# A two-layer attention and state-space step on one Trainium2 core: three gating blocks taken in turns, and the S5 read-out placed later among the weight units

## What is computed

```python
def _s5_layer(x, cond, p, init, return_state):
    h, gate = _pre(x, cond, g, w_ada, b_ada)
    u, z = jnp.split(h @ w_in, 2, axis=-1)
    ...
    hfr, hfi = _s5_scan(ug, a_re[0], ...)             # forward in time
    hbr, hbi = _s5_scan(ug[:, ::-1], a_re[1], ...)    # backward in time
    y = _s5_readout(hfr, hfi, ...) + _s5_readout(hbr, hbi, ...)[:, ::-1]
    y = y.reshape(bsz, l, D_MODEL) + d_skip * uf
    y = jax.nn.gelu(y)
    y = y * jax.nn.sigmoid(y @ w_glu + b_glu)         # the gating product
    out = (y * jax.nn.silu(z)) @ w_out
    x_new = x + gate * out
```

## Time and profile before

| | |
|---|---|
| median of 3 runs | 1264.6 us (1262.93 to 1269.76) |
| profiled execution | 1265.03 us, of which its span 1263.2 us |
| busy share of the span | PE 89%, DVE 60%, ACT 46%, POOL 18% |
| mean granted clock of PE | 0.942 of full speed |
| the chain that ended last | PE 65%, DVE 15%, DMA 9%, ACT 7%, issue 3% |

### The profile page before, as it was taken

How to read it: one execution, slowest core, us unless ns; L and a number is a source line. 1 busy time by engine, 2 the same in 40 slices (tenths; PEclk the granted TensorE clock), 3 DMA queues, 4 the chain that set the end, 5 groups by cost and what they waited for, 6 DMA issues and landing times.

```text
span 1263.2 us, 17442 instructions
## 1 busy us (share of the span) xinstructions
PE 1125.0 (89%) x6802; PEld 846.3 (67%) x6802; DVE 762.2 (60%) x1285; ACT 576.0 (46%) x808; POOL 222.1 (18%) x386
## 2 busy tenths in 40 slices
PE   4776999999999999999899969999697968799994
PEld 0224677677777777888667657788586856687883
DVE  3004776566656665787588745379676974365554
ACT  1313534434343444445434354565658475254443
POOL 2000222034202230331232230221020202100000
PEclk9866999999999999999999979999798978899998
DMA  9996789688969895666788775787272936754551
GB/s 355 422 394 250 261 319 336 258 335 320 349 256 347 311 354 204 209 219 214 286 336 330 289 269 207 244 289 241 105 262 90 298 106 231 270 196 167 178 189 66
DMA packets 60034, 327.21 MB, mean 259 GB/s; under 512 B 8800, under 2 KB 11616, under 8 KB 27952
## 3 DMA queue, kind: packets, MB, share of 16 engines
q1 hardware_dynamic: 38816, 262.44, 55.8%
q0 software_dynamic: 14224, 53.16, 12.3%
q10 hardware_dynamic: 6912, 10.49, 2.3%
HBM read 295.65 MB, written 30.41 MB: 258 GB/s over the span
## 4 chain that ended last, share of the span: by engine, by line
PE 65%; DVE 15%; DMA 9%; ACT 7%; issue 3%; ACTq 0%; SPq 0%; POOL 0%; DVEq 0%
PE ps L703 17%; PE ps L705 16%; PE ps L704 16%; DMA raw<-in_wada 6%; PE ps L601 5%; DVE wlo L1339 4%; DVE sb L1443 4%; DVE t L1438 3%; ACT whi L968 2%; PE ps L812 1%; PE ps L660 1%; PE ps L688 1%; PE ps L645 1%; DMA raw<-in_w 1%; PE ps L841 1%
## 5 line engine op out<-in xcount | busy, mean ns | idle before, releaser
L1339 DVE TENSOR_TENSOR wlo<-raw,whi 128x1024 fp32r<-128x1024 f32 x288 | 352.2, 1226 | 358.3 <-ACT whi L968 354.9
L968 ACT ACTIVATE whi<-raw 128x1024 fp32r<-128x1024 f32 x288 | 303.5, 1058 | 484.9 <-PE ps L705 469.5
L703 PE MATMUL ps<-whi,xhi 128*128 128x512 f32 x1152 | 477.3, 414 | 3.5 <-DVE xlo L1358 3.5
L704 PE MATMUL ps<-wlo,xhi 128*128 128x512 f32 x1152 | 456.2, 396 | 0.0
L705 PE MATMUL ps<-whi,xlo 128*128 128x512 f32 x1152 | 456.1, 396 | 0.0
L703 PEld LDWEIGHTS ps<-whi,xhi 128*128 128x128 f32 x1152 | 221.2, 192 | 78.5 <-issue 20.3
L705 PEld LDWEIGHTS ps<-whi,xlo 128*128 128x128 f32 x1152 | 220.4, 191 | 49.0
L704 PEld LDWEIGHTS ps<-wlo,xhi 128*128 128x128 f32 x1152 | 221.2, 192 | 46.2 <-issue 3.9
L601 PE MATMUL ps<-raw,cT 128*32 128x512 f32 x256 | 52.6, 929 | 31.7 <-DMA raw<-in_wada 31.5
L1443 DVE TENSOR_TENSOR sb<-sb,t 128x128 f32<-128x128 f32 x256 | 69.0, 290 | 6.6
L601 PE MATMUL ps<-araw,cT 128*32 128x512 f32 x512 | 61.5, 598 | 0.0
(11 more groups left out here) (205 smaller groups left out, 1077.1 us busy)
## 6 DMA issues: line engine op xcount, KB each, us to landing
raw<-in_w SPq DMA_DIRECT2D x144, 1024.0 KB, 5.0
araw<-in_wada SPq DMA_DIRECT2D x64, 1024.0 KB, 8.3
raw<-in_wada SPq DMA_DIRECT2D x32, 1024.0 KB, 8.7
btab_scratch<-bs ACTq DMA_DIRECT2D x32, 256.0 KB, 4.2
ctab_scratch<-ce POOLq DMA_DIRECT2D x16, 512.0 KB, 7.2
btab<-btab_scratch SPq DMA_DIRECT2D x16, 512.0 KB, 4.3
ctab<-ctab_scratch POOLq DMA_DIRECT2D x16, 512.0 KB, 4.7
par<-in_par POOLq DMA_DIRECT2D x32, 128.0 KB, 6.0
```

The source lines that it names most:

```text
L703: mm(acc, xhi[:, kt, st], whi[:, s, k], start=kt == 0, stop=False)
L704: mm(acc, xhi[:, kt, st], wlo[:, k0 // 2 % 4, k0 % 2, k], start=False, stop=False)
L968: af(whi[:, k % 4].rearrange("p k c -> p (k c)"), src, ACT.Copy).then_inc(s_hi, 1)
L1339: tt(wlo[:, g % 4, k % 2].rearrange("p k c -> p (k c)"), src, whi[:, k % 4].rearrange("p k c -> p (k c)").bitcast(F32), ALU.subtract).then ...
```

## The change

The budget's rules change in two numbers: the `hy` copies of a group start two units behind its last scan step, not one, and the sums of group w + 2 start four units behind those copies (`k + 6`, where the copies are at `k + 2`), not one. The gating blocks 28, 29 and 30 are taken in turns of two units. Block 30 then needs two more banks of PSUM while 28 and 29 hold theirs: it gets banks 4 and 5, slices 0, 1 and 2 of `Y` pass through banks 5, 7 and 4, the slices behind them all through bank 7, and every read-out uses bank 6 (those of groups 2 and 3 used bank 4, as the transposed final states did). Waits are adapted to that.

Worked out from the code, the tables of units are:

| | before | after |
|---|---|---|
| first sums, w = 0 to 3 | 176, 184, 197, 207 | 176, 184, 201, 209 |
| first `hy` copies | 196, 206, 219, 227 | 197, 205, 222, 230 |
| first read-out | 200, 210, 222, 230 | 201, 209, 225, 233 |
| transposes of slices 3 to 7 | 226, 230, 231, 234, 235 | 226, 231, 233, 238, 240 |
| unit that needs slices 3 to 7 | 229, 232, 233, 236, 237 | 231, 236, 237, 242, 243 |
| last scan step | 226 | 228 |
| steps of two groups at once / alone | 32 / 64 | 24 / 80 |

```diff
-B_PAIR = B_GLU
+B_TURNS = B_GLU
@@ scan_plan
                 if done[w] == NCH:
-                    ends[w] = k + 1
+                    ends[w] = k + 2
                     if w + 2 < NW:
-                        sums[w + 2] = k + 2
+                        sums[w + 2] = k + 6
@@
-X_AT = {226: 3, 230: 4, 231: 5, 234: 6, 235: 7}
-YZ_AT = (230, 231, 235, 236)
+X_AT = {226: 3, 231: 4, 233: 5, 238: 6, 240: 7}
+YZ_AT = (230, 231, 236, 241)
@@ place
-    j = k - UB * B_PAIR
-    if 0 <= j < 2 * UB:
-        return B_PAIR + j // 2 % 2, 2 * (j // 4) + j % 2
+    j = k - UB * B_TURNS
+    if 0 <= j < 3 * UB:
+        return B_TURNS + j // 2 % 3, 2 * (j // 6) + j % 2
@@ new functions
+def acc_bank(b):
+    return 4 if b == B_TURNS + 2 else 2 * ((b + (b > B_TURNS + 2)) % 2)
+
+def x_bank(n):
+    if n // TG == STAGES.index(B_TURNS):
+        return (5, 7, 4)[n % TG] if n % TG < AHEAD else 7
+    return 5 + n % 3
@@ PE, transposed
                 if g >= AHEAD:
-                    pe.wait_ge(s_xlo, n - AHEAD + 1)
+                    pe.wait_ge(s_xlo, n - AHEAD + 1 if i != 3 else n - 1 if g == AHEAD else n)
@@ PE, unit
-                if u == 0 and b >= 2:
-                    wait_evacuated(pe, b - 2)
+                if u == 0 and b == B_TURNS + 2:
+                    pe.wait_ge(s_xlo, TG * STAGES.index(B_TURNS) + AHEAD)
+                elif u == 0 and b >= 2:
+                    wait_evacuated(pe, b - 3 if b in (B_TURNS + 3, B_TURNS + 4) else b - 2)
@@ PE, ahead of the gating and of the output blocks
                 if u == 0 and b == B_GLU:
                     pe.wait_ge(s_uTsb, 2 * NW)
                     pe.wait_ge(s_Ssb, 4 * 4 * NW)
-                    pe.wait_ge(s_ysb, 8)
+                if u == 0 and b == B_OUT1:
+                    wait_evacuated(pe, B_TURNS + 2)
+                    pe.wait_ge(s_fso, 1)
```

More of the change, by code:

```diff
@@ L148, in ahead @@
     b, u = k // UB, k % UB
-    if b in (B_PAIR, B_PAIR + 1):
+    if B_TURNS <= b < B_TURNS + 3:
         return (X_AT[k],) if k in X_AT else ()
     return (u + AHEAD,) if b in STAGES and u + AHEAD < TG else ()
+def acc_bank(b):
[4 more added lines that the diff above has]
+    return 5 + n % 3
 def stage(k):
@@ L684, in transposed @@
                 if g >= AHEAD:
-                    pe.wait_ge(s_xlo, n - AHEAD + 1)
+                    pe.wait_ge(s_xlo, n - AHEAD + 1 if i != 3 else n - 1 if g == AHEAD else n)
                 for k in range(2):
                     for st in range(NS):
-                        last = tr(ps[:, 5 + n % 3, (2 * k + st) * P:(2 * k + st + 1) * P],
+                        last = tr(ps[:, x_bank(n), (2 * k + st) * P:(2 * k + st + 1) * P],
                                   src[:, st, (2 * g + k) * P:(2 * g + k + 1) * P], ident[:])
@@ L701, in unit @@
                     for st in range(NS):
-                        acc = ps[:, 2 * (b % 2) + st]
+                        acc = ps[:, acc_bank(b) + st]
                         mm(acc, xhi[:, kt, st], whi[:, s, k], start=kt == 0, stop=False)
@@ L830, in s5_outputs @@
                     pe.wait_ge(s_uTsb, 2 * NW)
-                if n == 8:
-                    pe.wait_ge(s_Ssb, 4 * 4 * NW)
-                out = [[y_bank(n)[e * M2:(e + 1) * M2, k * M2:(k + 1) * M2] for e in range(2)] for k in range(4)]
+                out = [[ps[e * M2:(e + 1) * M2, 6, k * M2:(k + 1) * M2] for e in range(2)] for k in range(4)]
                 for k in range(4):
@@ L857, in s5_beside @@
                     for ri in range(2):
-                        last = tr(ps[:, 4, ri * P:(ri + 1) * P], fs[:, ri], ident[:])
+                        last = tr(ps[:, 6, ri * P:(ri + 1) * P], fs[:, ri], ident[:])
                     last.then_inc(s_fsT, 1)
@@ L984, in high @@
                             kt = 2 * g + k
-                            x = ps[:, 5 + n % 3, (2 * k + st) * P:(2 * k + st + 1) * P]
+                            x = ps[:, x_bank(n), (2 * k + st) * P:(2 * k + st + 1) * P]
                             last = af(x, x, ACT.Identity, bias=shT[:, i // 2, kt, st:st + 1],
@@ L989, in high @@
                     act.wait_ge(s_tact, done)
-                af(xhi[:, 2 * g:2 * g + 2].rearrange("p k s c -> p (k s c)"), ps[:, 5 + n % 3], ACT.Copy).then_inc(s_xhi, 1)
+                af(xhi[:, 2 * g:2 * g + 2].rearrange("p k s c -> p (k s c)"), ps[:, x_bank(n)], ACT.Copy).then_inc(s_xhi, 1)
             def evacuate_in0(b):
@@ L1005, in evacuate_in0 @@
                 for st in range(NS):
-                    af(qkvz[:, j, st], ps[:, 2 * (b % 2) + st], ACT.Silu if j == 3 else ACT.Copy).then_inc(s_evA, 1)
+                    af(qkvz[:, j, st], ps[:, acc_bank(b) + st], ACT.Silu if j == 3 else ACT.Copy).then_inc(s_evA, 1)
             def attention(hb, j, u):
@@ L1085, in s5_outputs @@
                 act.wait_ge(s_y, n + 1)
-                bank = ps[:, 6 if n < 8 else 4, 0:4 * M2]
+                bank = ps[:, 6, 0:4 * M2]
                 dst = ys[:, :, 64 * q:64 * q + 64].rearrange("p t (r c) -> p t r c", r=4)
@@ L1112, in s5_beside @@
                     act.wait_ge(s_y, 4 * NW)
-                    af(fso[:].rearrange("p i c -> p (i c)"), ps[:, 4, 0:2 * P], ACT.Copy).then_inc(s_fso, 1)
+                    af(fso[:].rearrange("p i c -> p (i c)"), ps[:, 6, 0:2 * P], ACT.Copy).then_inc(s_fso, 1)
             for k in range(-4, NU):
@@ L1143, in _ @@
                         for st in range(NS):
-                            af(ub[w % 2][:, st], ps[:, 2 * (b % 2) + st], ACT.Copy).then_inc(s_evA, 1)
+                            af(ub[w % 2][:, st], ps[:, acc_bank(b) + st], ACT.Copy).then_inc(s_evA, 1)
                     if b == B_IN1 + NW:
@@ L1150, in _ @@
                         for st in range(NS):
-                            af(WA[:, st, c0:c0 + BN], ps[:, 2 * (b % 2) + st], ACT.Silu).then_inc(s_evA, 1)
+                            af(WA[:, st, c0:c0 + BN], ps[:, acc_bank(b) + st], ACT.Silu).then_inc(s_evA, 1)
                     if B_OUT0 <= b < B_IN1 or b >= B_OUT1:
@@ L1357, in low @@
                 dve.wait_ge(s_xhi, n + 1)
-                tt(xlo[:, 2 * g:2 * g + 2].rearrange("p k s c -> p (k s c)"), ps[:, 5 + n % 3],
+                tt(xlo[:, 2 * g:2 * g + 2].rearrange("p k s c -> p (k s c)"), ps[:, x_bank(n)],
                    xhi[:, 2 * g:2 * g + 2].rearrange("p k s c -> p (k s c)").bitcast(F32), ALU.subtract).then_inc(s_xlo, 1)
@@ L1418, in residual @@
                 for st in range(NS):
-                    tt(buf[:, st], ps[:, 2 * (b % 2) + st], gate[:, st, c0:c0 + BN], ALU.mult).then_inc(s_evV, 1)
+                    tt(buf[:, st], ps[:, acc_bank(b) + st], gate[:, st, c0:c0 + BN], ALU.mult).then_inc(s_evV, 1)
                 wait_evacuated(dve, b)
```

4 lines of the change are left out of this document (1 added, 3 removed).

## The result

| | before | after |
|---|---|---|
| median of 18 runs each | 1267.45 us | 1271.24 us |
| lowest to highest | 1262.93 to 1271.13 | 1265.16 to 1276.18 |
| profiled execution, its span | 1265.03, 1263.2 | 1266.58, 1264.8 |
| busy share PE, DVE, ACT, POOL | 89, 60, 46, 18% | 89, 60, 45, 17% |
| mean granted clock | 0.942 | 0.939 |

The changed kernel takes 1.0032 of the time, with an interval of 1.0017 to 1.0046: slower by 0.3%, less than the bound of 0.5% that the chances went by, and just above the range of 1256 to 1271. Of the 8.2 us between the forecast of 1263.0 and the measured 1271.24, 2.9 are the yardstick (the kernel before drew 1267.45 in these 18 runs, where three runs had given 1264.6), 3.8 are the loss, and 1.6 the gain that the forecast had counted on.

A forecast was written before the change was run, and what follows sets the result against it. PE, DVE and ACT were all near their limits, so the order of waits counts. From 1265.03, less 7.3 by unit 224 and plus 5.4 to unit 248, came 1263.1, stated as 1263.0 us, no change; range 1256 to 1271.

The forecast's parts named there:

- The stretch from unit 205 to 213: PE from 932.0 to 974.3: units, read-outs, sums, a 3.2 us wait for GELU and 1.8 of clock behind it.
- The second sums: Group 2's second sums: PE's 10.47 us wait goes; waits for GELU of 5.8 and 3.2 come at second read-outs.
- The lead of 7.3 us at unit 224: DVE's iteration 213 starts at 979.2, its 42.7 us chain ends at 1021.9, so `xlo` for unit 224 is 7.3 us earlier.
- the price of 1.8 for the second wait: Low PE clock behind the 3.2 us wait for group 1's GELU, counted as 1.8 us ahead of unit 213.
- the clock stays down longer: Rival: clock low through units 203 and 211 whole, 2.7 us each, and 1.5 for read-outs between: 1267.7 us; chance 0.08.
- Units 224 to 248: Work 82.9 us plus waits for `Y` and read-outs and 8.0 of clock: 106.3, 5.4 us more than before.
- trip 14.1 less two units: Slice 4, ahead of unit 231: HBM trip of 14.1 us less 5.4 of cover leaves an 8.7 us wait, where 2.63 was.
- the wait at slice 6: Ahead of unit 238: group 3's trip of 12.3 less three units' 8.4 leaves 3.9 us, where 6.67 was.
- The trip of group 2: Rival: group 2's trip takes as long as group 1's, 9.9 us more at unit 231: 1272.9 us; chance 0.10.
- At nothing: Items priced at zero: lone scan steps, one bank for slices 3 to 7, SP's and POOL's queues, waits at 228, 248, 256.
- the rival of dearer switches: Rival: each ACT table switch costs twice its 1.28 us row, ahead of the GELU waits: 5.1 later, 1268.1 us; chance 0.02.
- The turns: Gating blocks: the place of the transposes, not the turns of three, gives the 8.7 us wait at slice 4.

The follow-up runs named there:

- slices later: Changed kernel with slices 4 to 7 of `Y` transposed ahead of units 233, 235, 239, 241, not 231, 233, 238, 240: 1264.7 us, 0.9995 of the kernel before.
- `Y` ahead: Changed kernel with POOL loading group 2 of `Y` ahead of group 3's table loads, not behind them: 1269.29 us, 1.0028 of the kernel before.
- both: Changed kernel with slices 4 to 7 ahead of units 233, 235, 239, 241 and group 2's `Y` loaded ahead of the table: 1262.37 us, 0.9960.
- plan alone: Kernel before, turns of two, with only the later plan (copies k + 2, sums k + 6) and slices 6, 7 at 235, 236: 1296.63 us, 1.0239.
- sums late: Changed kernel with `hy` copies back at one unit behind the scan, sums still four behind them (k + 1, k + 5): 1267.78 us, 0.9995.
- `hy` late: Changed kernel with `hy` copies still two units behind the scan, but sums one unit behind them (k + 2, k + 3): 1262.9 us, 0.9961.
- all three edits: Changed kernel with sums at k + 3, slices 4 to 7 at 233, 235, 239, 241, and `Y` loaded ahead of group 3's last table: 1258.52 us, 0.9936.
- the old plan with `Y` first: Turns of three with the old plan (k + 1, k + 2), and group 2's `Y` loaded ahead of group 3's last table: 1262.37 us, 0.9984.
- mixed plan: Turns of three, slices at 233, 235, 239, 241, copies at k + 1, only group 2's sums four units behind them: 1266.42 us, 0.9991.
- the turns alone: Changed kernel's turns, banks and slice places with the old plan (k + 1, k + 2): 1260.53 us, 0.9948; once more, 1261.81 us, 0.9953.

## Why the prediction failed, step by step

Two terms of the sum were too small. The stretch from unit 205 to 213 took 46.12 us, not 42.3, and with it most of the forecast lead went; the wait for `Y` at slice 4 was 13.42, not 8.7. A third part of the miss, 2.9 us, is the yardstick.

**The second sums, right.** The 10.47 went, and PE stood for GELU at the second read-outs of groups 0 and 1. The first wait was forecast as 5.8 and came as 5.70. DVE's chain to unit 224 was 42.70 us against 42.7, without a gap.

**The lead of 7.3 us at unit 224, wrong by 4.6.** Counted from unit 197, iteration 213 of DVE was due 97.6 us behind it (979.2 less 881.65) and started 102.1 behind it (981.10 less 878.97). The term that failed is the stretch from unit 205 to 213: 42.3 forecast, 46.12 measured (930.04 to 976.16), 3.8 of the 4.6. Of these 2.4 are the clock: the price of 1.8 for the second wait had the clock back up early in unit 211, while units 211 and 212 took 15.62 (960.54 to 976.16) and not 13.2. All twelve weight matmuls of unit 211 ran at half clock (about 5.4 us instead of 2.7, the granted clock of the whole unit was 0.70), and unit 212 at 1.00. The 0.8 of wait too much is ACT, which left the copies of the sums 1.4 later than forecast: group 0's last GELU started 0.9 late, and the four store issues took 3.26, not 2.9. Around unit 203 the rest was lost: from the first GELU's wait to unit 205 20.85, not 20.4. This is what the rival "the clock stays down longer" named, with its unit 211 right in kind, and unit 203 less so (7.72 us where 6.6 is full clock, and 1.6 of it were counted already).

How far this is the plan's and how far chance, five kernels with the same order of work up to unit 224 show. The lead at unit 224 is 2.71 (the changed kernel), 5.08 (slices later), 2.70 (`Y` ahead), 2.50 (both), and 0.88 (plan alone). Unit 211 took 9.05, 6.59, 9.00, 8.91 and 9.08. So in this order of work the low clock behind a wait of 4 to 5 us is the common case and not the certain one, and the lead to expect is 1 to 3 us. The Trainium skill (TensorE: Matmul & The Clock Gate, What's actually happening) calls the count of half-rate matmuls variable from run to run of one kernel, and speaks there of a kernel's start; behind these waits, in five kernels with the same order of work, the traces show the same.

**Units 224 to 248, 106.3 forecast and 107.83 measured.** The mechanism was right: slice 4, ahead of unit 231, comes two units behind the read-out that it needs through HBM. Its size was off. The term "trip 14.1 less two units" gave a wait of 8.7, and it was 13.42, as the trip took 19.1. Against that the wait at slice 6 was 2.25, not 3.9 (trip of group 3 10.8, not 12.3), and work and waits at 101.6 (82.9, and 13.42, 1.51, 1.53, 2.25) leave 6.2 for the clock, where 8.0 was counted. That the whole came within 1.5 us is luck in part: 4.7 too little at slice 4 stand against 1.8 too much for the clock and 1.6 too much at slice 6. Sliding the slices confirms the mechanism: with two units more and `Y` ahead of the table, the wait is 5.23.

**The trip of group 2.** The rival took group 1's 14.7 as the length of a store and gave it 0.10; half of it came true. By the profiles it goes with the plan and with POOL's order, one execution of each kernel. The slowest of the four stores took 10.9, 12.8, 9.9, 11.5 and 11.3 us in the changed kernel, slices later, plan alone, sums late and `hy` late, all with a late plan and the table loaded ahead of `Y`; 7.4, 7.3 and 7.8 in the three late plans with `Y` loaded first (`Y` ahead, both edits, all three edits); 5.5, 5.0, 5.7 and 6.3 in the kernel before and the three with the old plan and the old order; 5.0 in the old plan with `Y` first; 8.0 in the mixed plan. With the table behind `Y` it is shorter by 3.5, 5.5 and 3.5 us in the three pairs of late plans (of which the third differs in its slices too), and hardly at all in the old one. Why the old plan's stores land in 5 to 6 us beside the same load stays open: issues of stores and table lie alike in both (stores 1042.40, table 1042.92 before; 1048.15 and 1048.67 after), and the DMA engines were less busy after, not more (0.63 of their time from 1047 to 1062, where it was 0.97 from 1040 to 1055). In the changed kernel they were busy for only 0.19 of the last 3.5 us ahead of POOL's load (1058.0 to 1061.5), while the last store was still waited for.

**At nothing.** The one bank for slices 3 to 7, SP's queue and the waits ahead of units 248 and 256 cost nothing visible in the changed kernel: the waits for `xlo` at the slices are 0.5 us. In other plans the one bank does show: such a wait is 2.76 with the turns alone and 3.55 with the late sums. A table load took 1.28 at 907.37, with GELU at 908.67, so the rival of dearer switches falls. The Trainium skill (ScalarE: Activation LUTs, What ACT_TABLE_LOAD costs) has 1380 ns of drain beside the load; 0.02 us lie behind this one, so the trace agrees on the load alone. The forecast's last step was rounded: 1263.1 less 0.4 is 1262.7, which changes nothing here.

**The turns.** The prediction put them at no gain or loss of their own: "it is the place of the transposes, not the turns of three, that gives this". True for the loss. But it did not ask what the turns would give under the old plan, 0.5%, and so did not see that the plan was what spent it.

## What to carry over

Where two edits are made at once, price each beside the other's absence: here one is worth 7 us and the other costs 11, and the sum is a loss of 4 that looks like next to nothing. A transfer through HBM that is waited for is priced with the slowest of its stores, and a consumer that could stand later should, since moving the transposes by one or two units, and one queue entry, gave back most of the loss (1.0032 to 0.9960, where the turns alone stand at 0.9948). Taking back one number of the plan, the four units for the sums, gave as much (0.9961). Taking a long wait off one engine, without shortening the chain that ends last (here DVE's 42.7 us), mostly gives it a new name.

## What was not expected of the hardware

Behind a wait of 4.0 to 5.0 us PE ran all twelve weight matmuls of the next unit at half clock in four of five executions of the same instructions (the unit took 8.9 to 9.1 us), and none of them in the fifth (6.59). A shorter wait shows the same: ahead of unit 256 every one of the fourteen executions waits 3.04 or 3.05 us for the same `xlo`. In seven of them, those of the kernel before and of the changed one among them, it cost nothing behind; in the other seven the first units ran partly at half clock and 1.6 us were lost, as here in the kernel with the slices later:

```profile
1154.46 0.63 PE L700 MATMUL ps<-ident,WA 128*128 128x128 f32 x4 [3.05 <-DVE xlo L1368]
...
1155.56 0.63 PE L719 MATMUL ps<-whi,xlo 128*128 128x512 f32 x1
```

So the prediction's "0 to 1.8" for a wait near 3 us is right, and one trace could not tell which.

A store of 128 KB took 4.5 us or 10.9 us from issue to landing within one group of four issued in 2.9 us. The slowest of the group took 10 to 13 us in the five late plans with the table first, and 5.0 to 6.3 us in the five executions with the old plan.
